# Strassen's seven products for half of two column groups of the attention's output projection, and a later place for the second half of x's rows

## What is computed

```python
# layer 0
h = rmsnorm(x) @ w_in                 # q, k, v, gate: 4 x 2048 columns
o = differential_attention(q, k, v)   # 8 heads
x = x + (headnorm(o) * silu(gate)) @ attn_w_out      # 256x2048 @ 2048x2048
# layer 1
h = rmsnorm(x) @ conv_w_in            # a, g, z: 3 x 2048 columns
u = depthwise_conv31(a * sigmoid(g)); u = silu(layernorm(u)) * silu(z)
x = x + u @ conv_w_out
return rmsnorm(x, final_gain)
```

## Time and profile before

| | |
|---|---|
| median of 3 runs | 823.15 us |
| the profiled execution's own time | 823.21 us |
| its span in the profile | 821.4 us |
| PE busy | 813.1 us (99%) |
| DVE busy | 660.0 us (80%) |
| ACT busy | 460.3 us (56%) |
| POOL busy | 236.3 us (29%) |
| moved by DMA | 175.22 MB, mean 213 GB/s |

### The profile page before, as it was taken

How to read it: one execution, slowest core, us unless ns; L and a number is a source line. 1 busy time by engine, 2 the same in 40 slices (tenths; PEclk the granted TensorE clock), 3 DMA queues, 4 the chain that set the end, 5 groups by cost and what they waited for, 6 DMA issues and landing times.

```text
span 821.4 us, 13877 instructions
## 1 busy us (share of the span) xinstructions
PE 813.1 (99%) x5614; PEld 752.1 (92%) x5614; DVE 660.0 (80%) x1111; ACT 460.3 (56%) x600; POOL 236.3 (29%) x115
## 2 busy tenths in 40 slices
PE   9999999999999999999999999999999999999996
PEld 9988899889998899888888899999999999998885
DVE  6578794797658784798788987999999999569782
ACT  7756643647336543656554455455664555597562
POOL 0400010000000000002000008989889888680000
PEclk9999999999999999999999999999999999999999
DMA  9995599966654556534656556556556555556842
GB/s 329 394 385 184 184 284 359 309 184 205 216 192 153 172 195 217 189 117 154 218 192 205 191 176 229 188 191 198 192 177 205 176 187 202 180 209 228 310 149 102
DMA packets 104137, 175.22 MB, mean 213 GB/s; under 512 B 3808, under 2 KB 41200, under 8 KB 103536
## 3 DMA queue, kind: packets, MB, share of 16 engines
q1 hardware_dynamic: 99712, 163.65, 58.2%
q0 software_dynamic: 2720, 8.39, 4.5%
q10 hardware_dynamic: 1648, 2.40, 0.8%
HBM read 172.30 MB, written 12.09 MB: 224 GB/s over the span
## 4 chain that ended last, share of the span: by engine, by line
PE 94%; DMA 3%; SPq 1%; ACT 1%; DVE 1%; issue 0%; ACTq 0%
PE ps_acc L1404 16%; PE ps_acc L1406 16%; PE ps_acc L1407 16%; PE ps_acc L1390 13%; PE ps_acc L1392 13%; PE ps_acc L1393 13%; DMA sb_xs<-in_x 2%; DMA sb_w_raw<-in_attn_w_in 1%; SPq L386 1%; SPq L388 1%; PE ps_a L1366 0%; PE ps_d L1494 0%; PE ps_d L1492 0%; PE ps_a L1506 0%; PE ps_a L1508 0%; PE ps_d L1493 0%
## 5 line engine op out<-in xcount | busy, mean ns | idle before, releaser
L536 ACT ACTIVATE sb_w_hi<-sb_w_raw 128x2048 fp32r<-128x2048 f32 x142 | 271.3, 1919 | 210.9 <-PE ps_acc L1407 140.1
L927 DVE TENSOR_TENSOR sb_w_lo<-sb_w_raw,sb_w_hi 128x2048 fp32r<-128x2048 f32 x97 | 220.3, 2289 | 80.5 <-ACT sb_w_hi L536 80.1
L491 POOL TENSOR_TENSOR sb_w_lo<-sb_w_raw,sb_w_hi 128x2048 fp32r<-128x2048 f32 x45 | 208.0, 4630 | 253.2 <-ACT sb_w_hi L536 253.2
L1404 PE MATMUL ps_acc<-sb_conv_hi,sb_w_hi 128*128 128x256 f32 x768 | 213.1, 277 | 0.0
L1407 PE MATMUL ps_acc<-sb_conv_hi,sb_w_lo 128*128 128x256 f32 x768 | 212.2, 276 | 0.0
L1406 PE MATMUL ps_acc<-sb_conv_lo,sb_w_hi 128*128 128x256 f32 x768 | 212.2, 276 | 0.0
L1162 DVE SCALAR_TENSOR_TENSOR ps_d<-sb_uT,sb_dwT,ps_d 128x256 f32<-128x256 f32 x480 | 189.0, 493 | 4.5 <-ACT ps_d L779 4.5
L1390 PE MATMUL ps_acc<-sb_w_hi,sb_act_hi 128*128 128x512 f32 x384 | 149.7, 390 | 0.0
L1392 PE MATMUL ps_acc<-sb_w_lo,sb_act_hi 128*128 128x512 f32 x384 | 149.6, 390 | 0.0
L1393 PE MATMUL ps_acc<-sb_w_hi,sb_act_lo 128*128 128x512 f32 x384 | 149.4, 389 | 0.0
L1406 PEld LDWEIGHTS ps_acc<-sb_conv_lo,sb_w_hi 128*128 128x128 f32 x768 | 144.2, 188 | 0.0
(11 more groups left out here) (210 smaller groups left out, 891.0 us busy)
## 6 DMA issues: line engine op xcount, KB each, us to landing
sb_w_raw<-in_attn_w_in SPq DMA_DIRECT2D x59, 1024.0 KB, 7.0
sb_w_raw<-in_conv_w_in SPq DMA_DIRECT2D x64, 512.0 KB, 4.5
sb_w_raw<-in_attn_w_out SPq DMA_DIRECT2D x16, 1024.0 KB, 5.0
sb_w_raw<-in_conv_w_in SPq DMA_DIRECT2D x16, 1024.0 KB, 5.0
sb_w_raw<-in_conv_w_out SPq DMA_DIRECT2D x15, 1024.0 KB, 5.1
weight_sums<-in_conv_w_out POOLq DMA_DIRECT2D x6, 1024.0 KB, 11.3
sb_w_raw<-weight_sums SPq DMA_DIRECT2D x4, 1024.0 KB, 5.8
sb_w_raw<-in_attn_w_in SPq DMA_DIRECT2D x15, 256.0 KB, 4.4
```

Of the source, the lines that this page charges most:

```text
L491: pool.tensor_tensor(w_part(w_lo, c), w_raw[c % RING][:], w_part(w_hi, c).bitcast(F32), ALU.subtract).then_inc(lo_ready_pool, 1)
L536: act.activation(w_part(w_hi, c if like is None else like), w_raw[slot][:], ACT.Copy).then_inc(hi_ready, 1)
L927: dve.tensor_tensor(w_part(w_lo, like), w_raw[slot][:], w_part(w_hi, like).bitcast(F32), ALU.subtract).then_inc(lo_ready, 1)
L1404: pe.matmul(into, left_hi, hi[:, kt], start=(kt == 0 and f % 2 == 0), stop=False, skip_group_check=True)
```

## The change

- The attention's output projection follows `OUT_CHUNKS` too: groups 0 and 3 as before; of groups 1 and 2 the first two chunks each as before, and the other four chunks become seven products of 12 matmuls. So it has 19 chunks in place of 16.
- x is put into PSUM by ACT before groups 1 and 2 (`fill_acc`), ACT scales the operand's second half in place (`m_scale`), DVE makes five sums of it, ACT and DVE split them, ACT copies the bank that gathers T1, T2 and B12 out after each of the three (`copy_m_bank`).
- POOL makes eight more DRAM sums (of `attn_w_out`), ahead of those of `conv_w_out`, and the low parts of six of the stage's chunks (`POOL_AMONG`: the 4th, 7th, 9th, 11th, 16th and 18th of the 19) in place of one.
- The turns and splits of x's groups stand at other places in the programs of DVE and ACT.
- At the start the second half of x's rows is loaded behind chunk 7, ACT makes chunk 7's high part before it squares that half, and DVE its low part before the norm's factor.

```diff
-CHUNKS_OUT = CHUNKS_ATT + NCH * PAIRS
+CHUNKS_OUT = CHUNKS_ATT + NCH * PAIRS + 3
-POOL_SEAM = CHUNKS_ATT + RING - 1
+POOL_AMONG = [CHUNKS_ATT + OUT_CHUNKS.index(what) for what in ((0, 3), (1, 1), (2, 0), (2, 1), (3, 0), (3, 2))]
...
-                        if first and t == 1 and i in (1, 2):
-                            st = i - 1
+                        if first and t == 1 and i in (1, 3):
+                            st = i // 2
                             sp.dma_start(xs[:, st], x_rows[:, st]).then_inc(rows_landed[st], 16)
...
                 act.wait_ge(ss_ready, st + 1)
                 if st == 0:
-                    high_part(RING + 2, 2, 2)
+                    for i in (2, 3):
+                        high_part(RING + i, i, 2)
...
             high_of_q(0)
-            high_part(RING + 3, 3, 2)
...
+            m_high(3)
+            hi_after((0, 0))
+            fill_acc(1)
+            hi_after((0, 1))
+            m_scale(2)
+            hi_after((0, 2))
+            m_scale(3)
+            hi_after((0, 3))
+            fill_acc(2)
+            for n, i in enumerate((S3, S0, S4, S6, S2)):
+                m_sum_high(n, i)
+            squares(0)
+            hi_after((1, 0))
+            copy_m_bank(T1, 0)
+            hi_after(T1)
+            x1_high(0)
+            hi_after((1, 1))
+            hi_after(B21)
+            hi_after((2, 0))
+            act.wait_ge(m_sum_lo, 5)
+            copy_m_bank(T2, 1)
+            hi_after(T2)
+            hi_after((2, 1))
+            copy_m_bank(B12, 2)
+            hi_after(B12)
+            hi_after(T4)
+            hi_after(B22)
+            hi_after(T3)
+            squares(1)
+            act.wait_ge(acc_free, 4 + 2 * (G_OUT + 3))
+            x1_high(1)
+            hi_after((3, 0))
+            squares(2)
+            x1_high(2)
+            hi_after((3, 1))
+            hi_after((3, 2))
+            squares(3)
+            hi_after((3, 3))
             x1_high(PAIRS - 1)
...
-            for i in range(1, NCH - 1):
+            for i in range(1, NCH):
                 low_part(RING + i, i)
             dve.wait_ge(ss_ready, 2)
...
+            m_low(3)
+            low_after((0, 0))
+            low_after((0, 1))
+            low_after((0, 2))
+            a11, a12, a21, a22 = m_rows()
+            dve.wait_ge(m_scaled, 8)
+            dve.tensor_tensor(m_raw_sums[S3], a12, a11, ALU.subtract).then_inc(m_sum_ready, 1)
...
+            add_rows(0)
+            low_after((0, 3))
+            for n, i in enumerate((S3, S0, S4, S6, S2)):
+                m_sum_low(n, i)
+            low_after((1, 0))
+            x1_turn(0)
+            low_after(T1)
+            x1_low(0)
+            low_after((1, 1))
+            low_after(B21)
+            dve.wait_ge(x1_copied, 1)
+            dve.tensor_tensor(x1_of(1, 0), m_partial[0], acc[:, 2], ALU.add).then_inc(acc_free, 1)
+            low_after((2, 0))
+            low_after(T2)
+            low_after((2, 1))
+            low_after(B12)
+            low_after(T4)
+            product_done(dve, T4, att_chunk)
+            dve.wait_ge(x1_copied, 3)
+            dve.tensor_tensor(x1_of(1, 1), acc[:, 3], m_partial[2], ALU.subtract).then_inc(acc_free, 1)
+            x1_turn(1)
+            low_after(B22)
+            product_done(dve, B22, att_chunk)
+            dve.tensor_tensor(x1_of(2, 0), acc[:, 0], m_partial[1], ALU.subtract).then_inc(acc_free, 1)
+            dve.tensor_tensor(x1_of(2, 1), acc[:, 1], m_partial[2], ALU.add).then_inc(acc_free, 1)
+            low_after(T3)
+            product_done(dve, T3, att_chunk)
+            for st, add in enumerate((ALU.subtract, ALU.add)):
+                dve.wait_ge(acc_free, 4 + 2 * (G_OUT + 2) + st + 1)
+                dve.tensor_tensor(x1_of(2, st), x1_of(2, st), bank_a[0][:], add).then_inc(x1_last, 1)
+            x1_low(1)
+            low_after((3, 0))
+            x1_turn(2)
+            low_after((3, 1))
+            x1_low(2)
+            low_after((3, 2))
+            add_rows(3)
+            x1_turn(3)
+            low_after((3, 3))
             x1_low(PAIRS - 1)
...
+                own(chunk_of((1, 0)), 1, 0, hi, lo)
+                times(chunk_of(T1), bank_a[1][:], rows(0, 0), start=True)
+                own(chunk_of((1, 1)), 1, 1, hi, lo)
+                times(chunk_of(B21), acc[:, 2], sums(S3))
+                if chunk_of is att_chunk:
+                    pe.wait_ge(x1_filled, 4)
+                else:
+                    pe.wait_ge(y_ready_pre, 6)
+                own(chunk_of((2, 0)), 2, 0, hi, lo)
+                pe.wait_ge(bank_copied, 1)
+                times(chunk_of(T2), bank_a[1][:], sums(S0))
+                own(chunk_of((2, 1)), 2, 1, hi, lo)
+                pe.wait_ge(bank_copied, 2)
+                times(chunk_of(B12), bank_a[1][:], sums(S4))
+                times(chunk_of(T4), acc[:, 3], sums(S6))
+                times(chunk_of(B22), acc[:, 0], sums(S2))
+                times(chunk_of(T3), bank_a[0][:], rows(1, 1), start=True)
```

More of the change, by code:

```diff
@@ new lines, in m_scale, with squares @@
+            def m_scale(n):
+                act.wait_ge(m_split, 4 * (n + 1))
+                for kt in range(4 * n, 4 * n + 4):
+                    act.activation(mT[:, kt], mT[:, kt], ACT.Copy, scale=vecs[:, G_HEAD, kt:kt + 1]).then_inc(m_scaled, 1)
+            def squares(n):
+                x1_done(act, n)
+                for st in range(ST):
+                    if n >= 2:
+                        act.wait_ge(ss_ready, ST + 2 * (n - 2) + st + 1)
+                    act.activation(squared[:, n % 2, st], xs[:, st, n * GW:(n + 1) * GW], ACT.Square,
+                                   accum_out=ss[:, 4 * st + n:4 * st + n + 1]).then_inc(ss_ready, 1)
@@ L1524, in _, with times @@
                 pair_slot(PAIRS - 1, i)
-            for i in range(NCH * PAIRS):
-                c, n = CHUNKS_ATT + i, i // NCH
-                if i < NCH:
-                    pe.wait_ge(m_split, CK * (i + 1))
+            def times(c, into, left, start=False):
                 low_part_ready(pe, c)
-                if i % NCH == 0:
-                    pe.wait_ge(acc_free, 2 * (G_OUT + n + 1))
-                project(c, i % NCH, n % 2, act_hi, act_lo)
+                high, low = w_part(w_hi, c), w_part(w_lo, c)
+                for k in range(CK):
+                    pe.matmul(into, left[0][:, k], high[:, k], start=start and k == 0, stop=False,
+                              skip_group_check=True)
+                    pe.matmul(into, left[0][:, k], low[:, k], start=False, stop=False, skip_group_check=True)
+                    ins = pe.matmul(into, left[1][:, k], high[:, k], start=False, stop=(k == CK - 1),
+                                    skip_group_check=True)
+                ins.then_inc(w_free, 1)
@@ new lines, in own, with two_groups, rows @@
+            def own(c, n, i, hi, lo):
+                low_part_ready(pe, c)
+                project(c, i, n % 2, hi, lo, filled=True)
+            def two_groups(chunk_of, hi, lo, sums, bank_copied):
+                def rows(st, a):
+                    return [part[:, 8 + a * CK:8 + (a + 1) * CK, st * P:(st + 1) * P] for part in (hi, lo)]
+                own(chunk_of((1, 0)), 1, 0, hi, lo)
[4 more added lines that the diff above has]
+                    pe.wait_ge(x1_filled, 4)
+                else:
+                    pe.wait_ge(y_ready_pre, 6)
[8 more added lines that the diff above has]
+                times(chunk_of(T3), bank_a[0][:], rows(1, 1), start=True)
@@ L1609, in _ @@
             pe.wait_ge(y_ready_pre, 2)
[L1610 to L1623 removed]
+            two_groups(out_chunk, conv_hi, conv_lo, sums, copied)
             for st in range(ST):
```

223 lines of the change are left out of this document (126 added, 97 removed).

## The result

| | before | after |
|---|---|---|
| median, us (lowest to highest, runs) | 823.15 (823.1 to 829.51, 5) | 838.76 (838.23 to 839.26, 5) |
| profiled execution: time, span, us | 823.21, 821.4 | 839.26, 837.5 |
| mean granted clock of TensorE | 1.00 | 0.99 |

The change makes the kernel slower: ratio 1.0189, 95% interval 1.0171 to 1.0207. Of the kernel before, one execution took 829.51 us; the other four lie within 0.12 us.

A forecast was written before the change was run, and what follows sets the result against it. PE's instructions (99% busy) were taken to set the time, with DVE's order deciding the changed stage. 823.2 + 13.0 (waits of 15.7 less the product's 2.73) - 0.9 for the start = 835.3 us, range 829 to 839.5.

The forecast's parts named there:

- the clock's rival: Output projection: PE's clock falls in the waits of 6.0 and 5.1 us, costing 3 us, 838.3 us; chance 0.20.
- The product saved: Output projection on PE: four chunks (96 matmuls) become seven products (84), -2.73 us.
- POOL and DVE exclude each other: Output projection: DVE's instructions with two SBUF inputs wait until POOL's low part ends, up to 4.6 us.
- the first rival: Output projection: POOL and DVE don't exclude each other, +7.3 us, time 829.6 us; chance 0.13.
- The waits: PE's six waits in and just behind the output projection: 0.4 + 6.0 + 1.1 + 1.8 + 1.3 + 5.1 = 15.7 us.
- The fourth conv chunk: Convolution's input projection: its fourth chunk waits for DVE's last split, +13.0 us, before the start's -0.9.
- The likeliest case: Whole kernel: the main forecast, with no fall of PE's clock, 835.3 us; chance 0.46.
- The start: Kernel's start: chunk 7 and x's second rows change places, PE's one wait goes, -0.9 us, bounds -0.9 and +1.5.
- The second batch of DRAM sums: Early in the kernel: eight more DRAM sums cost nothing, up to 2 us if the ring's cover fails in one slot.
- DVE's queue behind group 1's add: Output projection: DVE's work from group 1's last add to split 3 takes 44.7 us, with 38.3 available.
- The other side: Output projection: DVE keeps up, leaving only -2.7 and -0.9, 819.6 us; chance 0.05.

The follow-up runs named there:

- Experiment 3: Changed kernel with the low part of the stage's 7th chunk made by DVE in place of POOL: 836.19 us, ratio 1.0167.
- keep_clock2: Changed kernel with 24 and 20 calls of small unread products put on PE ahead of its two long waits: 836.28 us, ratio 1.0167.
- experiment 8: Changed kernel's operations reordered on ACT, DVE and POOL, on another chip, with the new start and the old one: 822.28 and 822.47 us.
- reordered2_old_start: Changed kernel's operations reordered on ACT, DVE and POOL, with the start of the kernel before: 822.47 us, ratio 0.9997.
- reordered3: Changed kernel's operations reordered so no POOL low part asks for the shared way during DVE's rows of splits: 819.68 us, then 819.9.
- reordered: Changed kernel's operations in a first other order on ACT, DVE and POOL, meant to leave nobody late: 828.11 us, ratio 1.0068.

## Why the prediction came out as it did

The forecast of 835.3 us was 3.5 short of the 838.76, and the range (829 to 839.5) held it, because its upper end was set by the clock's rival. Step by step:

- **The product saved, -2.73.** Right: 12 matmuls fewer, and a stage of 84.7 us once nobody is late.
- **POOL and DVE exclude each other for the whole overlap.** Right: 3.63 for a sum of 0.68, 5.16 for a low part of 2.29. Experiment 3 shows it by its effect, and takes the first rival (829.6) away.
- **The waits, 0.4 + 6.0 + 1.1 + 1.8 + 1.3 + 5.1 = 15.7.** Measured none, 5.7, none, 1.9, 1.1, 5.0 = 13.7. The 0.4 did not come. The 1.1 at the eleventh chunk (chunk 10 in the prediction) was swallowed by the half clock behind the 5.7, as `keep_clock2` shows, where it is back. The fourth conv chunk was forecast 13.0 - 0.9 = 12.1 us later and came 13.2 later: -1.0 for the start, -2.7 for the product, +13.7 of waits, +2.1 of half clock behind the first (matmuls 0.43 us apart and not 0.23, from 420.6 to 425.0), and 1.1 that is left. The starts of PE's matmuls show 0.8 of it at the restarts: before each of the four waits the profile's wait begins 0.16 us later than the spacing of starts would have it, and behind those of 1.9 and 1.1 the first matmul is followed 0.1 us late.
- **The clock.** This is the step that failed. The likeliest case had none; the rival that had it took 3 us for it, and the stretch behind the last wait cost 2.8. What happened is that rival, at 838.3. In the profiled execution (839.26) the forecast is 4.0 short: 1.1 of it at the fourth conv chunk, where the first stretch left 1.0, and 2.9 behind it, where the second cost 2.8. With the clock whole, in `keep_clock2`, that chunk starts 12.4 us later than before (493.41 against 481.0), with 12.1 forecast and 0.3 of its own later beginning: the sum without the clock was right. What would have tipped the balance was not in the trace of before, where PE never paused for more than 1.0 us. But both waits were forecast at over 5 us, and I gave too much to the case that only lacked a row against it.
- **The start, -0.9.** Mis-sized. The profiled execution has it (ACT 1.0 us earlier), the medians have not: -0.14 alone, and 0.2 between the two kernels of experiment 8. The wait at 44 us was 0.87 in the kernel before and 0.37 in `reordered2_old_start`. PE stood at the same place in both at 43 us, within 0.1 us, but the second half of x's rows came 0.45 us earlier in the second (ACT squares it from 35.17 and not 35.62): the length hangs on when the loads land, and one execution's 0.87 is no price. Also, in the twelve profiles with the new start PE is 0.15 to 1.4 us behind the kernel before by 12 us, and 0.1 in the one other with the old start. Whether the move itself costs that is not shown; it would explain why the medians gain so little.
- **The second batch of DRAM sums, 0.** Right: PE waits for nothing between 44 and 414 us. ACT's waits for loads from 95 to 250 us are 8.3 us where they were 11.0, and nobody behind it was late.
- **DVE's queue behind group 1's add, 44.7 us.** Right: from the end of that add at 449.2 to 494.0 it is 44.8, with one pause of 3.6 us for ACT where 3.5 was forecast.
- **The other side, DVE keeps up, 819.6.** Given 0.05, and right in that this order didn't. It is what the same operations do in `reordered3`, 819.7 and 819.9, in another order and with other low parts given to POOL. I had looked for the point that decides in the sum of DVE's work. It lies in the order, and in what stands under what: of DVE's 81.4 busy us after, 8.1 are the three meetings shown above (2.9, 2.9 and 2.2 beyond their length alone), and in `reordered3` POOL makes more of the low parts, eight in the stage, and costs DVE some 2.5 us there (DVE is busy 72.7 of 84.7 us).

## What to carry to other kernels

An engine at 80% that works in program order needs its queue written out against the clock of the engine that must not wait, not just summed up; that gave four of six waits to 0.3 us. In the profiled executions each pause of PE that lasted 3.5 us or more cost its own length and 1.5 to 3 us of half clock, and once a pause of 1.9 us cost 1.7; of that the part that a later wait would have taken anyway comes off, here 1.1 of 2.1 behind the first, and all that lies behind the last wait counts. And a low part handed to POOL helped here where DVE meanwhile turned or read PSUM, and hurt beside DVE's sums and splits: the same 12 matmuls saved, with the same start, came out at -3.3 us or +15.6, by the order and by who makes which low part.

## What the chip showed that I had not expected

- POOL with further low parts queued lets DVE in between them, one instruction at a time: four splits of 0.4 us each took 13.43 us, 4.8 for each of the middle two. In the other direction it isn't always so. In `reordered` a low part of POOL stood ready at 406.83 and took 6.89 us and not 4.6: it came in only behind three instructions of DVE in a row (to 409.2). The Trainium skill (SBUF — State Buffer, section "SBUF: two separate sides") gives the pair to whoever starts first, for one instruction; the trace agrees, with 4.82 us for a split beside a low part of 4.81.
- Between short DVE instructions the outcome is not settled: 3.25 us or 7.63 for the same eight splits, with POOL ready at the same point within 0.01 us, and some 2 us of the whole kernel. All 22 executions on one chip (with either start) took 821.9 us or more, seven of nine on another 820.2 or less. An order that comes out well in one profile can rest on such a meeting; a second chip showed it.
